# A two-layer diffusion backbone on one core: squares of the first norms added on VectorE, one pass for the differential matrix, bias tables prepared by GpSimd

## What is computed

```
def modulate(h, shift, scale):
    return rms_norm(h) * (1 + scale) + shift
...
    sh1, sc1, g1, sh2, sc2, g2 = adaln(c, w_mod[i], b_mod[i])      # silu(c) @ w_mod + b_mod
    ...
    out_l = mixer_diff_na(modulate(h, sh1, sc1), modulate(hc, csh1, csc1), ...)
...
def one_block(q_blk):                                             # differential heads
    s = einsum(q_blk, k) * scale
    p = softmax(s)
    a = p[:, :, 0] - lam * p[:, :, 1]
    return einsum(a, v)
...
return rms_norm(o) * subln_g * (1.0 - lam_init)
...
s_loc = einsum(q_r, k_nb) * scale + bias                          # neighbourhood heads
s = concatenate([s_loc, s_ctx]); p = softmax(s)
```

## Time and profile before

| | us |
|---|---|
| median of 3 runs | 3528.42 (3510.69 to 3531.58) |
| the profiled execution | 3510.3 |
| its span, first to last instruction | 3507.3 |
| first projection matmul starts | 64.40 |
| attention | about 269 to 453 |
| output projection, PEER, MLP, PEER | from 453 on |

### The profile page before, as it was taken

The page is one execution under the profiler, slowest core; times in us unless marked ns, Lnnn a source line. Parts: engine busy times, 40 slices in busy tenths (PEclk is TensorE's granted clock), DMA queues, the critical chain, the costliest instruction groups (busy, mean ns, idle before and its releaser), DMA issues.

```text
span 3507.3 us, 47345 instructions
## 1 busy us (share of the span) xinstructions
PE 3410.9 (97%) x18224; PEld 2958.9 (84%) x18224; DVE 2316.4 (66%) x4298; ACT 1222.3 (35%) x1634; POOL 1260.4 (36%) x746
## 2 busy tenths in 40 slices
PE   7999889999999999999999989999999999999998
PEld 3886568888888888999999768888888888999998
DVE  5778720894478723988887320895377723899987
ACT  3216633333455532222222333333355532222222
POOL 0000033454200002887773453454200002888872
PEclk9999989999999999999999999999999999999999
DMA  7771030344455556999996230344455555999995
GB/s 268 259 265 49 25 144 1 117 147 145 156 198 204 209 173 218 364 351 380 369 369 226 72 110 23 109 144 144 147 210 190 222 180 202 355 356 364 358 359 200
DMA packets 286133, 735.16 MB, mean 210 GB/s; under 512 B 33363, under 2 KB 116948, under 8 KB 266197
## 3 DMA queue, kind: packets, MB, share of 16 engines
q1 hardware_dynamic: 203988, 530.63, 43.0%
q0 software_dynamic: 45056, 134.38, 10.2%
q10 hardware_dynamic: 36864, 67.13, 5.0%
HBM read 612.48 MB, written 119.54 MB: 209 GB/s over the span
## 4 chain that ended last, share of the span: by engine, by line
PE 91%; DMA 2%; DVE 2%; POOL 2%; issue 1%; ACT 1%; SPq 0%; DVEq 0%; POOLq 0%; ACTq 0%
PE ps L1378 40%; PE ps L1416 26%; PE ps L1180 5%; PE ps L1331 5%; PE ps L1282 5%; PE ps L1391 2%; PE ps L1208 1%; PE ps L1240 1%; POOL picked L1501 1%; PE ps L1220 1%; DMA act<-act_scratch 1%; PE ps L1323 1%; PE ps L1131 1%; DMA Gin<-G_scratch 1%; PE ps L1091 0%
## 5 line engine op out<-in xcount | busy, mean ns | idle before, releaser
L1378 PE MATMUL ps<-xhi,Uhi 128*128 128x512 f32 x2048 | 808.1, 395 | 0.0
L1378 PE MATMUL ps<-xhi,Ulo 128*128 128x512 f32 x2048 | 799.0, 390 | 0.0
L1378 PE MATMUL ps<-xlo,Uhi 128*128 128x512 f32 x2048 | 797.2, 389 | 0.0
L1501 POOL DMA_INDIRECT picked<-act_scratch,aidx x256 | 373.5, 1459 | 985.0 <-DMA act_scratch<-act_st 907.5
L1416 PE MATMUL ps<-Hhi,Vhi 128*128 128x384 f32 x2048 | 687.9, 336 | 15.4 <-DVE Hlo L1991 15.4
L1416 PE MATMUL ps<-Hhi,Vlo 128*128 128x384 f32 x2048 | 686.1, 335 | 0.0
L1416 PE MATMUL ps<-Hlo,Vhi 128*128 128x384 f32 x2048 | 686.0, 335 | 0.0
L1029 ACT CAST Vhi<-Vraw 128x1024 fp32r<-128x1024 f32 x256 | 269.8, 1054 | 795.4 <-PE ps L1416 767.5
L1510 POOL DMA_INDIRECT vrow<-in_V,eidx x256 | 402.8, 1574 | 153.2 <-DVE acc L2004 87.6
L988 ACT ACTIVATE act_st<-ps 128x512 f32<-128x512 f32 x256 | 153.0, 598 | 871.6 <-PE ps L1378 531.2
L1378 PEld LDWEIGHTS ps<-xhi,Ulo 128*128 128x128 f32 x2048 | 384.5, 188 | 81.6
(11 more groups left out here) (276 smaller groups left out, 4539.3 us busy)
## 6 DMA issues: line engine op xcount, KB each, us to landing
Uraw<-in_UT SPq DMA_DIRECT2D x128, 1024.0 KB, 5.7
Vraw<-in_V SPq DMA_DIRECT2D x256, 512.0 KB, 6.3
act_scratch<-act_st ACTq DMA_DIRECT2D x256, 256.0 KB, 5.5
G_scratch<-G_st SPq DMA_DIRECT2D x24, 2048.0 KB, 8.3
act<-act_scratch SPq DMA_DIRECT2D x256, 192.0 KB, 6.5
Gin<-G_scratch SPq DMA_DIRECT2D x192, 256.0 KB
modw<-in_w_mod SPq DMA_DIRECT2D x80, 512.0 KB, 4.8
ring<-in_query SPq DMA_DIRECT2D x8, 2048.0 KB, 7.7
```

Of the source, the lines that this page charges most:

```text
L1378: mm = nc.tensor.matmul(up_bank(m), w, x[:, k, :], start=(k == 0 and j == 0), stop=(k == KT - 1 and j == 2))
L1501: nc.gpsimd.indirect_dma_start(picked[:, :, :].rearrange("p h k -> p (h k)")[:, p:p + 1], None, act_dram[layer].rearrange("m p (t o) -> (m ...
```

## The change

First stage: the squares go into the tiles of `xm` and `xc` themselves, so that ScalarE no longer waits for a free buffer; VectorE adds the 8 of them in 7 additions, each waiting for a square and for the addition before it, and TensorE sums over channels with one product. TensorE begins with the first set of modulation rows instead of the norm, and the columns of a set are made after the second product of the next set. On VectorE the context's norm stands ahead of the modulation. ScalarE loads the table of the root before the input lands.

Attention: the differential matrix is built without dividing by z0, which the RMS norm behind it removes, with epsilon times z0 squared in its place. GpSimd scales the bias tables (one instruction) and adds the mask (a second one), and VectorE only waits for `bias_ready`.

```diff
@@ squares(n, k)
-            return sq8[n % 2][k][:, :] if n >= 2 else sq0[:, k % 2, 0:NORMS[n][1]]
+            return sq8[n % 2][k][:, :] if n >= 2 else NORMS[n][2][:, k, :]
@@ ScalarE
-                    if n < 2:
-                        at_least(act_e, sq_used, n * KT + k - 1)
...
+            nc.scalar.activation(warm[:, :], ones[:, 0:1], ACT.Sqrt)
             act_e.wait_ge(h_in, 16)
-            stats(0)
-            row_to_sbuf(0)
-            row_to_sbuf(1)
+            stats(0, None, lambda: row_to_sbuf(0))
             act_e.wait_ge(ctx_in, 16)
-            stats(1)
+            stats(1, None, lambda: row_to_sbuf(1))
+            row_to_sbuf(2)
...
@@ TensorE, modulation_rows(n)
                 for k in range(KT):
+                    if k == 2 and n > 0:
+                        modulation_columns(n - 1)
...
@@ TensorE, norm(n)
-                width = NORMS[n][1]
-                for k in range(KT):
-                    pe.wait_ge(sq_ready, n * KT + k + 1)
-                    nc.tensor.matmul(ps[:, NORM_BANK[n], 0:width], ones[:, :], squares(n, k),
-                                     start=(k == 0), stop=(k == KT - 1)).then_inc(sq_used, 1)
+                pe.wait_ge(sq_added, n + 1)
+                nc.tensor.matmul(ps[:, NORM_BANK[n], 0:NORMS[n][1]], ones[:, :], squares(n, 0), start=True, stop=True
+                                 ).then_inc(sq_used, 1)
...
+            modulation_rows(0)
             norm(0)
-            modulation_rows(0)
             modulation_rows(1)
-            modulation_columns(0)

             pe.wait_ge(ms_ready, 1)
             norm(1)
-            modulation_columns(1)
             modulation_rows(2)
             modulation_rows(3)
-            modulation_columns(2)
             modulation_columns(3)
@@ GpSimd, ahead of mix_rest
+            pool.wait_ge(mask_ready, 1)
+            for h in range(HB // 2):
+                pool.wait_ge(bias_in[h % 2], 16 * (h // 2 + 1))
+                table = btab[h % 2][:, :, :, :].rearrange("p h s k -> p (h s) k")
+                nc.gpsimd.tensor_scalar(table, table, 1.0 / QK_SCALE, None, ALU.mult).then_inc(bias_scaled, 1)
+                pool.wait_ge(bias_scaled, h + 1)
+                nc.gpsimd.tensor_tensor(table, table, mask[:, :].unsqueeze(1).to_broadcast([P, 32, GRID_W]),
+                                        ALU.add).then_inc(bias_ready, 1)
@@ VectorE, stats(n), n < 2
-                dve.wait_ge(sq_used, (n + 1) * KT)
+                for k in range(1, KT):
+                    dve.wait_ge(sq_ready, n * KT + k + 1)
+                    ins = nc.vector.tensor_tensor(squares(n, 0), squares(n, 0), squares(n, k), ALU.add)
+                    if k < KT - 1:
+                        step(ins)
+                ins.then_inc(sq_added, 1)
+                dve.wait_ge(sq_used, n + 1)
...
             step(nc.vector.memset(zero_row[:, :], 0.0))
+            stats(1)
             modulation(0, sc1, g1, 2)
             scaled(0)
-            stats(1)
             scaled(1)
@@ VectorE, maxima(u)
                 if kind == "near" and qt == 0:
-
-                    dve.wait_ge(bias_in[h % 2], 16 * (h // 2 + 1))
-                    table = btab[h % 2][:, :, :, :].rearrange("p h s k -> p (h s) k")
-                    step(nc.vector.scalar_tensor_tensor(out=table, in0=table, scalar=1.0 / QK_SCALE,
-                                                        in1=mask[:, :].unsqueeze(1).to_broadcast([P, 32, GRID_W]),
-                                                        op0=ALU.mult, op1=ALU.add))
+                    dve.wait_ge(bias_ready, h + 1)
@@ VectorE, probabilities(u)
-                step(nc.vector.reciprocal(rz[:, j:j + 2], zs[:, j:j + 2]))
+                if kind == "diff":
+                    step(nc.vector.reciprocal(rz[:, j + 1:j + 2], zs[:, j + 1:j + 2]))
+                    step(nc.vector.scalar_tensor_tensor(out=nlr[:, u:u + 1], in0=rz[:, j + 1:j + 2],
+                                                        scalar=zs[:, j:j + 1], in1=lamv[:, 5:6],
+                                                        op0=ALU.mult, op1=ALU.mult))
+                else:
+                    step(nc.vector.reciprocal(rz[:, j:j + 2], zs[:, j:j + 2]))
...
-                    step(nc.vector.tensor_tensor(nlr[:, u:u + 1], rz[:, j + 1:j + 2], lamv[:, 5:6], ALU.mult))
-                    step(nc.vector.tensor_scalar(to, Ebuf[:, (j + 1) % 4, :], nlr[:, u:u + 1], None, ALU.mult))
-                    last = nc.vector.scalar_tensor_tensor(out=to, in0=Ebuf[:, j % 4, :], scalar=rz[:, j:j + 1],
-                                                          in1=to, op0=ALU.mult, op1=ALU.add)
+                    last = nc.vector.scalar_tensor_tensor(out=to, in0=Ebuf[:, (j + 1) % 4, :], scalar=nlr[:, u:u + 1],
+                                                          in1=Ebuf[:, j % 4, :], op0=ALU.mult, op1=ALU.add)
@@ VectorE, mean_squares()
-                nc.vector.tensor_scalar(oms[:, 0, :], osums, float(D // P), EPS, ALU.mult, ALU.add
-                                        ).then_inc(oms_ready, 1)
+                z0 = zs[:, 0:2 * HEAD_END:2]
+                step(nc.vector.scalar_tensor_tensor(out=oms[:, 1, :], in0=z0, scalar=EPS, in1=z0,
+                                                    op0=ALU.mult, op1=ALU.mult))
+                nc.vector.scalar_tensor_tensor(out=oms[:, 0, :], in0=osums, scalar=float(D // P), in1=oms[:, 1, :],
+                                               op0=ALU.mult, op1=ALU.add).then_inc(oms_ready, 1)
```

More of the change, by code:

```diff
@@ L381, in backbone @@
         sq_summed = sem("sq_summed")
+        sq_added = sem("sq_added")
         ms_ready = sem("ms_ready")
@@ L423, in backbone @@
         bias_used = sem("bias_used")
+        bias_ready = sem("bias_ready")
+        bias_scaled = sem("bias_scaled")
+        mask_ready = sem("mask_ready")
         bank_shared = sem("bank_shared")
@@ L850, in _ @@
                 split_in(i)
-            row_to_sbuf(2)
             row_to_sbuf(3)
@@ L1680, in _ @@
             step(nc.vector.tensor_scalar(lamv[:, 5:6], lamv[:, 4:5], -LAM_INIT, None, ALU.add))
-            step(nc.vector.tensor_scalar(mask[:, :], mask[:, :], 1.0 / QK_SCALE, None, ALU.mult))
+            nc.vector.tensor_scalar(mask[:, :], mask[:, :], 1.0 / QK_SCALE, None, ALU.mult).then_inc(mask_ready, 1)
             def maxima(u):
```

## The result

The changed kernel takes 3538.11 us, the median of 12 runs (3534.82 to 3542.70); the kernel before, run beside it on the same chip, 3523.79 (12 runs, 3510.69 to 3531.58). The ratio is 1.0043, with a 95% interval of 1.0031 to 1.0054: no change by the bound of 1%, and 14 us slower (11 to 19) by the interval. Forecast were 3535.5 us, and +7.1 us against before.

What follows compares the result with a forecast made beforehand. TensorE, busy 97% of the span, was taken as the bound. The terms -6.4 - 3.7 - 2.4 + 13.4 + 2.9 + 3.3 gave +7.1 us, so 3535.5 us from the 3528.42 us median; range 3500 to 3548.

Steps and rivals of the forecast that it cites:

- The forecast case: Attention: GpSimd and VectorE each wait for the other's whole instruction, so +7.1 us overall; chance 0.6.
- first stage: Start-up: VectorE's chain starts at 38.4 instead of 42.29 us, without the context's norm inside it; -6.4 us.
- first two tables' GpSimd work: Attention's first units: GpSimd's multiplications and additions hold up VectorE's small instructions, making TensorE late; +13.4 us.
- first table off VectorE: Change to the neighbourhood units: 2.1 us of waiting and 1.6 of low clock saved; -3.7 us.
- third table's GpSimd work: Unit 19: the two `Abuf` passes wait for GpSimd, so TensorE's transposes start later; +2.9 us.
- fourth table's GpSimd work: Unit 23: `Abuf` is held until 398.3 us and the transposes start at 398.4 instead of 395.10; +3.3 us.
- fourth table off VectorE: Later neighbourhood units: TensorE's waiting and low clock after VectorE's table pass are saved; -2.4 us.
- One pass for nothing: 16 differential units: one matrix pass saves VectorE 0.65 us each, but TensorE sets the pace, so no gain.
- A: Attention: the engines' mutual exclusion is not felt, only gains stand; -15.6 us, 3512.8 on the median; chance 0.24.
- B: Bias tables: GpSimd's multiplication takes twice the addition, 9.2 us; about +30 us, 3558; chance 0.06.
- C: Start-up gains nothing, as the norm waits behind the modulation rows; +6.4 us on top, 3542; chance 0.1.
- the 9.2 of the sum: Attention: gain from taking bias tables off VectorE if GpSimd's work disturbs nobody; -9.2 us together.

Runs made afterwards that it cites:

- first profile of before: The unchanged kernel's original profiled execution, no edit: span 3507.3 us, first projection at 64.40 us, attention stretch 184.05 us.
- second profile of before: The unchanged kernel run and profiled once more, no edit: 3524.5 us, first projection at 65.28 us, attention stretch 185.01 us.
- eighths: The changed kernel with each of GpSimd's eight table instructions cut into eight of 128x256: median 3509.87 us, ratio 0.9959 to the kernel before.
- sixteenths: The changed kernel with each GpSimd table instruction cut into 16 of 128x128: 3501.52 us, ratio 0.9955 to the kernel before.
- GpSimd's unrelated work: The kernel before plus GpSimd multiplications and additions on a 128x1024 tile that nobody reads: 3531.5 us against 3519.26 in its set.
- halves: The changed kernel with each GpSimd table instruction cut into 2 of 128x1024: attention stretch 185.62 us against 201.70 uncut.
- quarters on GpSimd: The changed kernel with each GpSimd table instruction cut into 4 of 128x512: attention stretch 182.93 us against 201.70 uncut.
- the kernel with the additions alone: The changed kernel without GpSimd's four multiplications, its four additions whole and the tables left unscaled: attention stretch 192.78 us.

## Why the forecast was right, and where it was off

The forecast case, the two engines excluding each other, is what happened: no change by 1%, and slower. The size was half of what was measured, +7.1 us against +14.3 on the medians. That the absolute time comes within 2.6 us of the forecast is in part luck: it was reckoned from a median of 3528.42, and the twelve runs have 3523.79. Against the first profile of before, read from where the products of each unit start:

| term | forecast, us | measured, us |
|---|---|---|
| first stage | -6.4 | -6.5 (-5.9 at the first scores) |
| first two tables' GpSimd work | +13.4 | +13.8 |
| first table off VectorE | -3.7 | -3.7 |
| third table's GpSimd work | +2.9 | +4.6 |
| fourth table's GpSimd work | +3.3 | +5.5 |
| fourth table off VectorE | -2.4 | -2.5 |

Against the second profile of before the first two rows are -7.4 and +12.7; the others move by at most 0.2.

**The first stage** was met by two errors that cancel: the chunk of `modall` came 0.7 us earlier than reckoned (16.71 instead of 17.4), and the first rows took 0.8 longer (9.35 instead of 8.55), so both end at 26.

**The mis-sized term** is GpSimd's multiplication: "it has one input and no row here: 2.3 (half) to 4.6; I take 3.5". It took 5.36 us, above the upper bound. I had bounded a one-input instruction by the two-input one of the same size, and that was no bound: here it is the dearer of the two (4.49 for the addition, forecast 4.6). The Trainium skill (GPSIMD Engine Reference, "Elementwise — side-by-side cycle accounting") gives 1.8 cycles an element as the best case of a tight loop. The estimate of 3.1 us made from it was further off still; the measurement decides. The 1.86 us too few explain the third and fourth table nearly alone (2.9 + 1.86 = 4.8, 3.3 + 1.86 = 5.2).

**The first two tables** came out within 0.4 us of the forecast (0.7 against the second profile), in part by two errors that cancel. The order forecast (multiply, `nmx` of unit 2; add, `nlr` of unit 1; multiply, the pass of unit 1; add, `nmx` of unit 3) is row for row the one in the trace. With the dearer multiplications the transposes of unit 2 came 13.8 us late instead of 11.8; but the 1.6 us added for the clock were not due. TensorE ran its slow products (2.77 us at 288.40) while it would have waited anyway, and was back at full clock at 294.91.

**The third table** held both `Abuf` passes, one behind each GpSimd instruction (10.39 us in the row). I had only let them wait together.

**One pass for nothing** was wrong. With the tables on VectorE it brings 2.9 us at the first table and 4.4 by unit 27, of which 2.5 go again in the last units. So the -3.7 at the first table is met in its number, while its cause is not shown: 2.9 of it come with the one pass alone, which the sum had at nothing, and what the table's move would bring with two passes was not run.

**The rest of the 14 us.** Start-up and attention give +11.7 of the median's +14.3 (interval 11 to 19) against the first profile of before and +9.2 against the second. Nothing in the later stages differs by more than one kernel's own repeats do, so the 2.6 to 5.1 us that are left over are not assigned.

**The rivals.** A (the lock is not felt) is refuted by the held rows, and its gain of 15.6 us is about what the kernel does reach once the pieces are short: 3509.9 in eighths, 13.9 under before. B had the right sign for the multiplication's price, far too large. C did not occur: the first modulation rows ended at 26.

**What became of the gain of moving the tables.** Between the sixteenths and the changed kernel lie 23.0 us of stretch: +11.3 by the second unit, +6.1 at the third table, +8.6 at the fourth, and 3.0 back at the end, where the TensorE of the sixteenths falls to its lower clock and that of the changed kernel does not. Without being held, moving the tables is worth 4.4 us (183.10 to 178.71), not the 9.2 of the sum, part of which the one pass has by itself, and cutting them up on VectorE is worth as much (178.95).

## What to carry to other kernels

Before moving work from VectorE to GpSimd, ask what VectorE will have to issue while a GpSimd instruction runs. What counted here is the length of one GpSimd instruction and how many VectorE instructions on the critical chain fall under one, and not GpSimd's total. If the move is to stay, cut GpSimd's instructions: here eight pieces turned the whole change from 14 us of loss into 14 us of gain, though GpSimd was busy 17 us more. Some 4 us of that gain are the tables' move; the rest is the first stage and the one pass. Take no bound for an instruction on GpSimd from the number of its inputs.

## What was unexpected of the hardware

- GpSimd's multiplication by a constant is slower than its two-input addition at every size: 5.36 against 4.49 us for 2048 elements, 0.53 against 0.44 for 128. The table gives about 2.5 and 2.1 ns an element, with some 0.2 us for each instruction.
- GpSimd's multiplication does not always hold to its end. The two-input pass at 282.96 of the changed kernel ended at 287.43, so its 1.02 us began at about 286.4, 1.9 us before the multiplication over it ended (288.35). `rspread`, at 396.78 with two inputs too, ended at 400.87, so its 0.69 us began at 400.2, again 1.9 us before the multiplication's end (396.69 + 5.36). By the same reckoning the additions let `nlr` and `nmx` in no more than 0.2 us before their end. One-input instructions show both: `nmx` at 273.53 was held to the end of the multiplication over it, but with GpSimd's unrelated work a one-input pass ran in its usual 0.62 us under a multiplication, behind a two-input `nlr` that got in 1.9 us before that one's end (two multiplications stand in the first row; the first ends at about 284.6). So "held for a whole instruction", as the prediction has it, is not exact for the multiplication. Which part of it lets VectorE in was not tried.

```profile
281.76 5.62 POOL L1536 TENSOR_SCALAR idle_tile<-idle_tile 128x1024 f32<-128x1024 f32 x2
281.86 0.95 DVE L1739 TENSOR_TENSOR nlr<-rz,lamv 128x1 f32<-128x1 f32 x1
282.84 0.62 DVE L1740 TENSOR_SCALAR Abuf<-Ebuf,nlr 128x768 f32<-128x768 f32 x1
```

- Fills hold one-input `TENSOR_SCALAR` passes on VectorE and leave two-input ones alone (0.63 and 1.15 held, 1.02 and 2.29 as without).
- TensorE's clock takes back part of a gain. With the tables in quarters on VectorE, and with halves, eighths or sixteenths on GpSimd, it falls to the lower level twice in the last 16 us of attention, and 24 products take 2.5 to 2.8 us instead of 1.53. With the tables whole on VectorE and one pass, and with quarters on GpSimd, it falls once there. The changed kernel and the three profiles with the attention of before and nothing added to it keep the full clock, though the idle entries are the same there (in the changed kernel 0.77, 0.77, 2.43 and 0.77 us, each for ScalarE's `ATbuf`). It does not go with the long holds alone: the kernel with the additions alone has them and falls too. Why stays open, and that the clock is the whole of the 3 us given back at the end was read from the rows and not tested.
